# Where the attention sums, the layer outputs and the first weight copy are issued in a two-layer decoder step

## What is computed

```python
def branch_inputs(x, g_norm, w_in, pos):
    z = rmsnorm(x, g_norm) @ w_in
    q, k, v, ga, bg, cg, hc, gc = jnp.split(z, SPLITS, axis=-1)
    q = rope(q.reshape(b, t, N_HEADS, HEAD_DIM), pos)
    k = rope(k.reshape(b, t, N_KV_HEADS, HEAD_DIM), pos)
    return q, k, v, ga, bg, cg * hc, gc
def branch_output(x, o_attn, ga, bg, conv_out, gc, w_out, p_i, w_pg, w_pp):
    mix = jnp.concatenate([o_attn * jax.nn.silu(ga), bg * conv_out * jax.nn.silu(gc)], axis=-1)
    x = x + mix @ w_out
    return x + jax.nn.sigmoid(x @ w_pg) * (p_i @ w_pp)
```

## Time and profile before

| what | value |
|---|---|
| median of three runs | 1155.0 us |
| the profiled execution | 1154.99 us |
| its span, first to last instruction | 1153.1 us |
| granted TensorE clock, mean | 0.999 |
| TensorE matmuls busy | 1141.4 us (99%) |
| VectorE busy | 675.4 us (59%) |
| ScalarE busy | 500.9 us (43%) |
| GpSimd busy | 500.2 us (43%) |
| DMA, mean rate | 61 GB/s |

### The profile page before, as it was taken

The page is one execution under the profiler, slowest core; times in us unless marked ns, Lnnn a source line. Parts: engine busy times, 40 slices in busy tenths (PEclk is TensorE's granted clock), DMA queues, the critical chain, the costliest instruction groups (busy, mean ns, idle before and its releaser), DMA issues.

```text
span 1153.1 us, 18898 instructions
## 1 busy us (share of the span) xinstructions
PE 1141.4 (99%) x7321; PEld 1126.5 (98%) x7321; DVE 675.4 (59%) x1230; ACT 500.9 (43%) x1129; POOL 500.2 (43%) x655
## 2 busy tenths in 40 slices
PE   8999999999999999999999999999999999999998
PEld 8999999999999999999999999999999999999997
DVE  3445868888845444455642476878785444444443
ACT  6322556666633221333322146575755322133334
POOL 4574446566643232222455434565656423222220
PEclk9999999999999999999999999999999999999999
DMA  8631111111111212111063311111111212211103
GB/s 241 173 94 55 37 38 37 38 38 37 38 43 56 73 39 69 47 46 42 19 185 85 82 38 38 37 38 37 38 38 38 67 50 57 65 47 46 47 1 151
DMA packets 125920, 70.44 MB, mean 61 GB/s; under 512 B 41108, under 2 KB 121828, under 8 KB 125800
## 3 DMA queue, kind: packets, MB, share of 16 engines
q1 hardware_dynamic: 122976, 63.43, 19.3%
q10 hardware_dynamic: 2856, 5.82, 2.1%
HBM read 59.10 MB, written 6.76 MB: 57 GB/s over the span
## 4 chain that ended last, share of the span: by engine, by line
PE 92%; DVE 6%; ACTq 1%; issue 1%; ACT 1%; POOL 0%; POOLq 0%
PE ring L469 82%; PE aux L507 2%; PE aux L483 2%; DVE yc L1309 2%; PE aux L492 1%; DVE up L1305 1%; PE aux L622 1%; DVE yc L1307 1%; DVE tmp L1252 1%; DVE raw L1226 0%; PE aux L563 0%; DVE kst L1209 0%; PE aux L595 0%; PE aux L556 0%; PE aux L725 0%
## 5 line engine op out<-in xcount | busy, mean ns | idle before, releaser
L469 PE MATMUL ring<-act,ws 128*128 128x352 f32 x6048 | 998.8, 322 | 1.1 <-POOL ws L450 1.1
L469 PEld LDWEIGHTS ring<-act,ws 128*128 128x128 f32 x6048 | 965.7, 188 | 4.8 <-POOL ws L450 1.4
L450 POOL TENSOR_TENSOR ws<-stage,ws 128x256 fp32r<-128x256 f32 x352 | 282.7, 835 | 513.5 <-ACT ws L782 513.5
L791 ACT ACTIVATE act<-tmp 128x352 fp32r<-128x352 f32 x120 | 59.7, 497 | 233.9 <-DVE tmp L1348 143.7
L444 POOL TENSOR_TENSOR stage<-stage,gT 128x256 f32<-128x256 f32 x208 | 143.5, 721 | 26.4 <-DMA stage<-in_w_in_dram 23.5
L782 ACT ACTIVATE ws<-stage 128x1024 fp32r<-128x1024 f32 (+1 forms) x84 | 91.6, 1090 | 42.4 <-PE ring L469 20.2
L1073 DVE TENSOR_TENSOR act<-tmp,act 128x352 fp32r<-128x352 f32 x120 | 71.8, 599 | 54.1 <-ACT act L791 53.4
L1371 DVE TENSOR_TENSOR tmp<-ring,gate 128x352 f32<-128x352 f32 x48 | 25.2, 524 | 85.6 <-ACT gate L1007 85.6
L423 POOL TENSOR_SCALAR_AFFINE_SELECT pw<-pw 128x512 fp32r<-128x512 f32 x56 | 39.3, 704 | 71.1 <-ACT pw L937 63.5
L1346 DVE TENSOR_TENSOR tmp<-ring,act 128x352 f32<-128x352 f32 x48 | 25.2, 525 | 66.8 <-PE ring L469 66.8
L469 PE MATMUL ring<-pT,ws 128*128 128x352 f32 x288 | 53.7, 322 | 0.0
(11 more groups left out here) (203 smaller groups left out, 1033.2 us busy)
## 6 DMA issues: line engine op xcount, KB each, us to landing
stage<-in_w_in_dram SPq DMA_DIRECT2D x36, 512.0 KB, 3.9
stage<-in_w_in_dram SPq DMA_DIRECT2D x32, 256.0 KB, 3.9
stage<-in_w_pg_dram SPq DMA_DIRECT2D x16, 512.0 KB, 3.8
rotq<-raw ACTq DMA_DIRECT2D x32, 132.0 KB, 2.5
xnat<-in_x_prompt_dram SPq DMA_DIRECT2D x8, 512.0 KB, 7.5
stage<-in_w_out_dram SPq DMA_DIRECT2D x32, 128.0 KB, 2.9
stage<-in_w_out_dram SPq DMA_DIRECT2D x16, 256.0 KB, 3.1
out_dram<-ynat SPq DMA_DIRECT2D x5, 512.0 KB, 2.7
```

Of the source, the lines that this page charges most:

```text
L450: rest = nc.gpsimd.tensor_tensor(ws[:, s, 1, k:k + 2, :], stage[:, s, k:k + 2, :], ws[:, s, 0, k:k + 2, :].bitcast(F32), ALU.subtract)
L469: mm = nc.tensor.matmul(out, ws[:, w % 2, wp, kw, :], x[:, xp, kx, cs], start=(i == 0 and wp == 0 and xp == 0), stop=(i == n - 1 and wp == 1))
L791: nc.scalar.activation(dst, tmp[:, s % 2, :], ACT.Copy).then_inc(S["hi_out"], 1)
```

## The change

Four edits:

1. The 13 DMAs of a layer's outputs leave ScalarE's queue. SyncE issues them before its load of the second `w_out` tile (tile number NA + 1 = 27 of the layer), behind a wait for `tail_taken`.
2. `take_o` of a slot stands right behind the operation that frees the slot's bank, ahead of `split_low`, the convolution or the product.
3. The high part of weight tile 0 is copied by VectorE, behind a wait for `w_scaled`, before it touches any block of x.
4. 8 instead of 14 idle turns behind the norm weights' turn.

```diff
@@ SyncE
                         sp.wait_ge(w_lo, w - 1)
                         sp.wait_ge(w_hi, w - 1)
+                    if f == NA + 1:
+
+                        sp.wait_ge(S["tail_taken"], 3 * (l + 1))
+                        ctail = comb[:].rearrange("p a n -> p (a n)")[0:2 + NS, :]
+                        out = S["tail_out"]
+                        sp.dma_start(new_conv_prompt[l, 0], ctail[0:2, :]).then_inc(out, 16)
...
+                        for r in range(DS):
+                            sp.dma_start(new_k_sample[l, :, WB - DS + r].rearrange("b g d -> b (g d)"),
+                                         ptcp[r:r + DS * (DB - 1) + 1:DS, 0, P:2 * P]).then_inc(out, 16)
+                            sp.dma_start(new_v_sample[l, :, WB - DS + r].rearrange("b g d -> b (g d)"),
+                                         vsmp[r:r + DS * (DB - 1) + 1:DS, :]).then_inc(out, 16)
                     if f < NA:
                         kind, j, c0 = A_TILES[f]
@@ TensorE
-            idle_turns(aux[:, 3, 0:P], 14)
+            idle_turns(aux[:, 3, 0:P], 8)
@@ ScalarE
                 nc.scalar.activation(act[0][:, 0, :, t0:t0 + n], src, ACT.Copy).then_inc(S["x_hi"], 1)
-                if b == 0:
-                    split_weights(0)
...
-                        sc.wait_ge(S["tail_taken"], 3 * (l + 1))
-                        out = S["tail_out"]
-                        sc.dma_start(new_conv_prompt[l, 0], ctail[0:2, :]).then_inc(out, 16)
...
@@ VectorE
             ve.wait_ge(const_made, 5)
+            ve.wait_ge(w_scaled, 1)
+            V.tensor_copy(ws[:, 0, 0, 0:KT, :], stage[:, 0, 0:KT, :]).then_inc(w_hi, 1)
             for b in range(NB + 1):
...
                     elif kind == "ga":
                         V.tensor_tensor(gate[:, s % 2, :], src, r, ALU.mult).then_inc(fr, 1)
+                    for u in at_slot(s, o=7):
+                        if u not in last:
+                            take_o(l, u)
                     if s == R_TABLES:
...
                         link(V.tensor_tensor(ytmp[:, c, :], ytmp[:, c, :], r, ALU.mult))
-                    for u in at_slot(s, o=7):
-                        if u not in last:
-                            take_o(l, u)
                     for u in at_slot(s, scores=0):
                         scores_of(l, u)
```

More of the change, by code:

```diff
@@ L319, in _ @@
                         sp.wait_ge(w_hi, w - 1)
+                    if f == NA + 1:
[3 more added lines that the diff above has]
+                        sp.dma_start(new_conv_prompt[l, 0], ctail[0:2, :]).then_inc(out, 16)
+                        for r in range(2):
+                            o = 2 + DS - 2 + r
+                            sp.dma_start(new_conv_sample[l, :, r, :], ctail[o:o + DS * (DB - 1) + 1:DS, :]).then_inc(out, 16)
+                        sp.dma_start(new_k_prompt[l, 0].rearrange("k g d -> k (g d)"), ptcp[:, 0, 0:P]).then_inc(out, 16)
+                        sp.dma_start(new_v_prompt[l, 0].rearrange("k g d -> k (g d)"), vlast[:]).then_inc(out, 16)
+                        for r in range(DS):
[3 more added lines that the diff above has]
+                                         vsmp[r:r + DS * (DB - 1) + 1:DS, :]).then_inc(out, 16)
                     if f < NA:
```

## The result

| what | before | after |
|---|---|---|
| median of four runs | 1155.01 us | 1171.99 us (1170.74 to 1173.18) |
| ratio | 1 | 1.0142 [1.0126, 1.0158] |
| the profiled execution | 1154.99 us | 1173.18 us |
| its span | 1153.1 us | 1171.2 us |
| granted TensorE clock, mean | 0.999 | 0.992 |

The change makes the kernel 17 us slower. 1171.8 was predicted, so sign and size were right. Where TensorE waits was not. Lines after the change: the group of a slot is L485, `turn` L508, `pv` L523, `take_o` L1229, `split_low` L1209 and L1212, `probs_low` L1220, ScalarE's move L946, the product of a gc slot L1335.

What follows compares the result with a forecast made beforehand. TensorE, busy 99% of the span, was taken to bound the kernel, with gaps of some 5 us to win. 1154.99 - 1.1 (edit 1) - 0.7 (edits 3 and 4) + 18.6 (edit 2) = 1171.8 us, range 1156 to 1181.

Steps and rivals of the forecast that it cites:

- What bounds the kernel: Whole kernel: TensorE is busy 99% of the span, so only gaps worth some 5 us can be won.
- Edit 1, -1.1: Slot 75 of layer 0: outputs on SyncE end TensorE's 1.07 us wait for weights, -1.1 us.
- rival E: SyncE needs over 16 us for 13 outputs, TensorE waits for tile 27 in both layers: above 1176 us, chance 0.03.
- Edits 3 and 4, -0.7: Start: slot 0 about 1.2 us earlier, but slot 2 waits for block 8 of x, ending at 24.60: -0.7 us.
- Edit 2, the lateness: Slots 35 and 37: VectorE idles 1.5 and 2.2 us before `take_o` for ScalarE's L932, 3.35 us late after slot 37.
- Edit 2, where it reaches TensorE: Slots 38 to 40: lateness passes without slack to `pv` of unit 4, margin 0.34 us; TensorE waits 3.1 us net.
- its own sign: Slot 42: wrong if `pv` starts without a wait, above all if VectorE isn't idle before `take_o` in slots 35, 37.
- Edit 2, the size: Units per layer: 3.1 + 0.9 + 4.2 + 0.7 + 0.4 = 9.3 us; both layers +18.6 us.
- Rival B, the idle GpSimd: Slot 35 and alike: moved pair runs beside idle GpSimd, so lateness is smaller: 1162 us, chance 0.12.
- Rivals C and D: C: lateness never reaches TensorE, 1150.8 us, chance 0.13. D: loss and gain cancel, 1155 us, chance 0.06.
- C's condition: Slots 35 and 37: ScalarE's L932 comes before the bank is free, leaving only the gains, 1150.8 us.
- the middle value: Edit 2: 9.3 us a layer, between bounds 4.4 and 13.9, the convolution losing beside L450 what the pair gains.

Runs made afterwards that it cites:

- the best version, experiment 12: Changed kernel, ScalarE's move of the half result ahead of the scaling, weight tile 1 split behind block 7 of x instead of block 6: 1150.01 us, 0.9957.
- experiment 7: Changed kernel, edit 2 in place, with ScalarE's move of the half result ahead of the scaling of the probabilities instead of behind SiLU: 1150.47 us, 0.9962.
- experiments 3 and 4: Kernel before with the early sum (edit 2) in one kind of slot only: hc slots 1158.9 us, 1.0031; gc slots 1164.68 us, 1.0082.
- experiments 9 to 12: Kernel before with edit 1 alone, 1154.45 us; edit 4 alone, 1153.39; changed kernel without edit 2, ScalarE's move early, 1155.75; with edit 2, tile 1 split later, 1150.01.

## Why the prediction was right, and where it was not

- **What bounds the kernel**, and that a change without matmuls wins only gaps: held. Of the 5 us of gaps the best version took 5.
- **Edit 1, -1.1.** The wait at slot 75 went, -1.32 in the profiled pair. Alone the edit gave 0.9993 [0.9984, 1.0001] over 11 runs, not told from nothing, and 0.8 to 1.4 us at like clock. Edit 4 ended the same wait without it. SyncE took 8.1 us for the 13 issues and the load behind them was in time, which ends rival E.
- **Edits 3 and 4, -0.7.** The mechanism (slot 2 hangs on block 8, which comes behind tile 1's split) held, and experiment 12 shows it: with the split later the wait is gone. The profiled pair gave -0.40, since block 8 came 0.3 us later than taken, and this is within what untouched starts differ by. Tile 1 was scaled from 18.99 on instead of 18.67. The copy took 0.69 us, where 1.1 was taken between 0.5 and 1.5; it was hidden all the same.
- **Edit 2, the lateness.** Idle times of 1.5 and 2.2 us forecast, 1.55 and 2.29 found; the cause is shown by experiment 7.
- **Edit 2, where it reaches TensorE: the step that failed.** The prediction walked from the lateness through slots 38 to 40 to `pv` of unit 4, with a margin of 0.34 us, and said that TensorE waits there. TensorE had met the same lateness earlier, at `turn` of unit 4, which waits for `probs_low` of unit 3. The walk followed data that flow forward through one unit, and left out that a bank is shared between neighbours. By its own sign ("I am wrong if TensorE's `pv` starts in slot 42 without a wait") this part was wrong:

```profile
205.35 0.69 DVE L1229 TENSOR_TENSOR raw<-aux,ptcp 64x512 f32<-64x512 f32 x1 [0.74 <-ACT ptcp L946]
...
206.87 1.09 PE L523 MATMUL aux<-pw,vsa 128*128 128x512 f32 x4
```

  The path through `pv` was real all the same: experiments 3 and 4 show TensorE waiting there, 0.65 and 0.66 us at unit 4. In the changed kernel the turn had already held TensorE longer, and half clock kept it 1.39 us longer still. `take_o` ends 0.83 us before `pv` of unit 4 starts, so without the half clock `pv` would have waited some 0.6 us (an estimate, 1.39 - 0.83). The size of the lateness held: 3.35 us forecast at the end of slot 37, 3.14 + 0.62 = 3.76 found against TensorE, and the 0.4 more is L1209's 1.12 in place of 0.68 us.
- **Edit 2, the size.** Units up to 5: +4.0 forecast, -0.40 to +4.44 = 4.8 found. Units 7 to 10: 4.9 against 4.44 to 8.24 = 3.8. Units 12 to 14: 0.4 against 0.7. Per layer 9.3 forecast, 9.3 and 9.05 found. That the sum fits so well is partly luck: the pieces are off by up to 1.1 us each and cancel, and part of the time found is half clock (1.4 us in layer 0, 1.5 + 2.3 us in layer 1), of which the prediction knew nothing. There it took the place of waits: from slot 52 to 62 the shift grows by 1.5 us in either layer, in layer 1 by half clock alone (+2.3, then -0.8), in layer 0 by the waits of units 9 and 11 (+2.0, then -0.5).
- **Rival B, the idle GpSimd.** In slot 35 the 64x512 subtraction (L1209) fell into GpSimd's idle time, but the pair behind it (L1212) only began there: at 176.03, where L466 starts at 176.20. It took 1.05 us, against 1.39 us before (174.69 there) and 0.60 beside an idle GpSimd. But the convolution behind it met L466 and took 3.39 us in all (0.92, 0.74, 1.73), where it took 2.38 us. The prediction had put it so: what the pair gains the convolution loses, and more. In slot 37 L1209 met a mask on top, which it had not foreseen: 1.12 us. The Trainium skill ("SBUF — State Buffer", Who interferes with whom) says that a VectorE instruction with two SBUF inputs contends with a GpSimd instruction that reads SBUF. The rows agree: 0.68 us became 1.12 us beside L439. Contention moved with the operations, as the middle value assumed.
- **Rivals C and D** are excluded by the interval. C's condition, that ScalarE's move come before the bank is free, is what experiment 7 makes true but for 0.59 us in slot 37. It gave 1150.5 us, where C had 1150.8.

## What to carry to other kernels

An instruction moved to the front of an in-order queue is early only if its input is. Otherwise the engine idles, and all that stood inside the old wait now stands behind the new one; look first at what the producer does just before, and move both or neither. To find where lateness reaches the bounding engine, list for each of its instructions every semaphore that it waits on, also those that only free a bank for the next unit, with its margin, and follow the lateness to the first whose margin is used up.

## What was not expected of the hardware

- **Half clock with a busy engine.** Stretches at a granted 0.5 appear after a wait of 2.49 us (190:196 above), but none after the wait of 3.46 us before unit 9 (the window 256:260 has 1.00). They also appear at the start of layer 1, from 589.5 on, right behind 18 matmuls of one column each. Timeline after:

```profile
587.24 2.17 PE L579 MATMUL aux<-ones,acc 128*128 128x1 f32 x18
589.27 3.09 PE L485 MATMUL ring<-act,ws 128*128 128x352 f32 x10
```

  Those 18 stand in every kernel. In the profile of edits 3 and 4 alone the window 577:589 has

```profile
577.00:589.00 12.00, 11.99 (x71) 11.70 (x70) 3.17 (x8) 3.46 (x6) 2.78 (x4) 0.86 0.86 274
```

  71 matmuls, where the kernel before has 81 in the same window. Of the profiles of all 14 kernels seven have the stretch and seven do not. A step of 1.3 to 1.9 us between groups of runs of one and the same kernel fits this: of the 27 runs of the kernel before beside experiments 9 to 12, 13 had a mean granted clock of 0.999 and a median of 1154.15 us, and 14 one of 0.997 or 0.998 and 1156.1 us. Where in the run the clock was lost only a trace shows. What decides whether the stretch comes was not found.
- **An issue's time varies.** The same DMA was issued in 1.79 us and in 0.44 us, in the same queue and place of two kernels, and in 0.44 us in layer 1 of both. These 1.35 us are the whole difference in ScalarE's idle time (9.81 against 8.46 us), and slot 75 waited in the one profile and not in the other.
- **A copy is faster than a subtraction.** VectorE's copy of 128x1024 from SBUF to SBUF took 0.69 us, its subtractions over as many columns (L1083, one operand in PSUM) 1.22 us. The Trainium skill ("VectorE: DVE Perf Modes", Mode 2×_2P) says that an operation with a single source in SBUF can use both read ports and give two results a cycle, and that one with two tensors, or with a source in PSUM, cannot. The two durations agree with that; no run here tells the two reasons apart.
